# A Strassen feed-forward on one core: block products in another order, a filter tap on ScalarE, a low part on VectorE

## The reference, cut to what matters

```python
def conv_ffn(h, w_in, conv_w, conv_b, w_out, pad):
    T = h.shape[1]
    u = h @ w_in
    up = jnp.concatenate([pad.astype(u.dtype), u], axis=1)
    c = conv_b + sum(up[:, j:j + T] * conv_w[j] for j in range(CONV_W))
    g, val = jnp.split(c, 2, axis=-1)
    y = (jax.nn.silu(g) * val) @ w_out
    return y, up[:, up.shape[1] - (CONV_W - 1):]
```

## Time and profile before

| | |
|---|---|
| median of 3 runs | 3251.47 us (3251.31 to 3253.42) |
| the profiled execution | 3248.83 us, its span 3247.0 us |
| busy share of the span | PE 92%, PEld 89%, DVE 67%, POOL 51%, ACT 38% |
| mean granted TensorE clock | 0.971 |
| feed-forward of layer 0, opening | 732 to 791 us |
| its 20 pairs | 791 to 1256 us |
| its down-projection | from 1262 us |

### The profile page before, as it was taken

How to read it: one execution, slowest core, us unless ns; L and a number is a source line. 1 busy time by engine, 2 the same in 40 slices (tenths; PEclk the granted TensorE clock), 3 DMA queues, 4 the chain that set the end, 5 groups by cost and what they waited for, 6 DMA issues and landing times.

```text
span 3247.0 us, 47471 instructions
## 1 busy us (share of the span) xinstructions
PE 2993.8 (92%) x18469; PEld 2876.1 (89%) x18469; DVE 2178.7 (67%) x3257; ACT 1238.0 (38%) x2590; POOL 1650.1 (51%) x1023
## 2 busy tenths in 40 slices
PE   7999999896999999999987999999699999999998
PEld 6888888796999998999977888889699999999997
DVE  6666666347888887335776777762888888833465
ACT  5555555223333332113340666651333333311243
POOL 2222221325899994222334778753499999622231
PEclk8999999898999999999988999999899999999999
DMA  5222222312222224211104121221122222422111
GB/s 113 69 68 72 68 66 91 104 40 73 70 73 68 73 67 152 101 60 55 39 24 121 34 59 51 94 82 46 64 69 73 70 70 72 156 79 78 59 39 62
DMA packets 284366, 237.37 MB, mean 73 GB/s; under 512 B 29988, under 2 KB 266228, under 8 KB 284148
## 3 DMA queue, kind: packets, MB, share of 16 engines
q1 hardware_dynamic: 269336, 220.43, 22.5%
q10 hardware_dynamic: 14812, 13.97, 1.4%
HBM read 170.20 MB, written 64.16 MB: 72 GB/s over the span
## 4 chain that ended last, share of the span: by engine, by line
PE 61%; DVE 13%; POOL 11%; issue 6%; ACT 5%; DMA 3%; SPq 0%; ACTq 0%; POOLq 0%; DVEq 0%
PE ps L1150 17%; PE ps L1152 16%; PE ps L1151 16%; POOL t L934 6%; PE ps L1333 2%; ACT t L1916 2%; PE ps L1468 2%; PE ps L1286 2%; PE ps L1269 2%; DVE t L2351 1%; POOL t L962 1%; POOL t L953 1%; PE ps L1353 1%; DVE t L2366 1%; DMA t<-in_w_ffn_in 1%
## 5 line engine op out<-in xcount | busy, mean ns | idle before, releaser
L1150 PE MATMUL ps<-t,t 128*128 128x384 f32 (+1 forms) x4760 | 1601.1, 336 | 136.9 <-POOL t L889 53.8
L1152 PE MATMUL ps<-t,t 128*128 128x384 f32 (+1 forms) x4760 | 1566.6, 329 | 0.0
L1151 PE MATMUL ps<-t,t 128*128 128x384 f32 (+1 forms) x4760 | 1565.3, 329 | 0.0
L1150 PEld LDWEIGHTS ps<-t,t 128*128 128x128 f32 x4760 | 903.8, 190 | 177.5 <-POOL t L889 55.5
L1151 PEld LDWEIGHTS ps<-t,t 128*128 128x128 f32 x4760 | 904.8, 190 | 1.0 <-issue 0.2
L1152 PEld LDWEIGHTS ps<-t,t 128*128 128x128 f32 x4760 | 903.2, 190 | 0.0
L934 POOL TENSOR_TENSOR t<-t,t 128x512 fp32r<-128x512 f32 x320 | 542.0, 1719 | 20.0 <-ACT t L2024 10.7
L889 POOL TENSOR_TENSOR t<-t,t 128x1024 fp32r<-128x1024 f32 x101 | 249.0, 2465 | 455.5 <-ACT t L1803 452.2
L2024 ACT ACTIVATE t<-t 128x512 fp32r<-128x512 f32 x320 | 198.0, 631 | 526.8 <-POOL t L942 218.8
L2698 DVE TENSOR_TENSOR t<-t,ps 128x384 f32<-128x384 f32 (+1 forms) x240 | 126.3, 531 | 279.6 <-PE ps L1152 279.6
L883 POOL TENSOR_TENSOR t<-t,t 128x1024 fp32r<-128x1024 f32 x51 | 106.0, 2079 | 266.5 <-PE ps L1152 266.0
(11 more groups left out here) (191 smaller groups left out, 4119.4 us busy)
## 6 DMA issues: line engine op xcount, KB each, us to landing
t<-in_w_ffn_in SPq DMA_DIRECT2D x160, 256.0 KB, 2.9
ff_dram<-t SPq DMA_DIRECT2D x44, 544.0 KB
t<-ff_dram SPq DMA_DIRECT2D x44, 544.0 KB, 6.8
t<-in_w_ffn_out SPq DMA_DIRECT2D x44, 512.0 KB, 3.4
t<-in_w_qkv_a SPq DMA_DIRECT2D x24, 512.0 KB, 3.9
t<-in_w_ple_gate SPq DMA_DIRECT2D x16, 512.0 KB, 3.8
out<-t SPq DMA_DIRECT2D x32, 192.0 KB, 2.1
t<-in_w_o_a SPq DMA_DIRECT2D x8, 512.0 KB, 4.0
```

The lines of the kernel that those rows point to most:

```text
L1150: pe.matmul(out, a_hi, b_hi, start=start, stop=False, skip_group_check=True)
L1151: pe.matmul(out, a_hi, b_lo, start=False, stop=False, skip_group_check=True)
L1152: return pe.matmul(out, a_lo, b_hi, start=False, stop=stop, skip_group_check=True)
```

## The change

- **PE's order in a pair** becomes A11, A11, S3, A21, A22, A22, S2, S1, A12, A12, S4. The steps of `blk_done` are renumbered with it: 4 is A22, 5 is S2, 6 is S1, 7 is A12, 8 is S4.
- **POOL** takes the low part of A22 right after that of A21, before S4; it no longer takes that of A12 (seven low parts in a pair). **DVE** takes it in `last_low`, between the gate filter and the gate. PE's A12 products wait for it.
- **The first tap** of both filters goes to ACT (`first_tap`: Identity with scale and bias over 1090 elements). In ACT's order the value tile's stands behind the highs of A22(n+1) and S2(n+1), the gate tile's at the head of the next pair. ACT's other steps are put in another order too.
- **SP** waits for step 4 (not 6) before it loads A22(n+1) and for step 7 (not 8) before A12(n+1). `store_tile(n + 1)` stays where it is.
- **Opening:** ACT copies and splits in another order, the fourth combination moves from POOL to DVE (`combined_fourth`) with its own buffers for each k (`t4_words`, four counters in place of one), POOL splits chunk c0+2 before it combines.
- **Down-projection:** the first four gated tiles come into `ff_first`, not `ff_raw[0]`, and are loaded after step 4 of the last pair; on DVE they come before the last value filter.

```diff
@@ SP, a pair
                         load_block("A21", n + 1)
                         store_tile(n + 1)
-                        sp.wait_ge(blk_done, BLK_DONE + done + 6)
+                        sp.wait_ge(blk_done, BLK_DONE + done + 4)
                         load_block("A22", n + 1)
-                        sp.wait_ge(blk_done, BLK_DONE + done + 8)
+                        sp.wait_ge(blk_done, BLK_DONE + done + 7)
                         load_block("A12", n + 1)
...
-                        sp.wait_ge(blk_done, BLK_DONE + done + 5)
-                        down_chunk(0, 1)
+                        sp.wait_ge(blk_done, BLK_DONE + done + 4)
                         sp.wait_ge(ff_stored, FF_STORED + 16 * (f0 + 8))
                         load_tiles(0)
+                        sp.wait_ge(blk_done, BLK_DONE + done + 6)
+                        down_chunk(0, 1)
@@ POOL, pair_weights
                 block_rest("A21", 2)
+                block_rest("A22", 4)
                 pool.wait_ge(blk_loaded["A12"], BLK_LOADED + 16 * (m + 1))
...
                 block_rest("S2", 5)
                 block_rest("S1", 6)
-                block_rest("A22", 4)
                 block_rest("S4", 8)
-                block_rest("A12", 7)
@@ POOL, ffn_weights and combine
                 split(c0 + 1, ffn=l)
+                split(c0 + 2, ffn=l)
                 combine(l, 0)
-                combine(l, 1)
-                split(c0 + 2, ffn=l)
-                combine(l, 2)
-                combine(l, 3)
                 split(c0 + 3, ffn=l)
+                for k in range(1, 4):
+                    combine(l, k)
...
+                if k == 3:
+                    stored, before = comb_stored[1]
+                    pool.wait_ge(stored, before + 32 * (l + 1))
...
-                pool.tensor_tensor(t4_raw, h21, t_raw[1][:, k, :], ALU.subtract).then_inc(comb_made, 1)
@@ ACT
+                def first_tap(unit, t, kind):
+                    n = t + NFF * kind
+                    act.wait_ge(pad_done, unit + 1)
+                    if t:
+                        act.wait_ge(ff_made, f0 + t)
+                    act.activation((cg, cv)[kind], ubuf[kind][:, 2:T + 4], ACT.Identity, scale=conv_c[l][:, n + 88:n + 89],
+                                   bias=conv_c[l][:, n + 132:n + 133]).then_inc(conv_step, 1)
@@ ACT, pair (the new order)
                     if n:
                         first_tap(unit - 1, n + 1, 0)
                         first_copied(n)
                         loaded_high("A12", n)
                         made_high("S4", n, 4)
                         sigmoid(n + 1, unit - 1)
                     if more:
                         loaded_high("A11", n + 1)
                         loaded_high("A21", n + 1)
                         made_high("S3", n + 1, 1)
                     act.wait_ge(blk_done, BLK_DONE + 8 * m + 4)
                     last_segment(ubuf[1], 6)
                     if more:
                         loaded_high("A22", n + 1)
                         made_high("S2", n + 1, 2)
                         first_tap(unit, n + 2, 1)
                         made_high("S1", n + 1, 3)
                     act.activation(ubuf[0][:, 2:386], ps[:, 0, 0:384], ACT.Copy).then_inc(u_kept, 1)
                     last_segment(ubuf[0], 5)
@@ DVE, filtered, gate_half and pair
-                    dve.wait_ge(pad_done, unit + 1)
-                    dve.tensor_scalar(dst, ub[:, 2:T + 4], col(88), col(132), ALU.mult, ALU.add).then_inc(conv_step, 1)
                     dve.wait_ge(conv_step, 3 * unit + 1)
...
+                    if n < PAIRS - 1:
+                        last_low(n + 1)
                     gate_tile(2 + n, unit)
...
+                def last_low(n):
+                    m = PAIRS * l + n
+                    hi, lo, raw = slots[l]["A12"]
+                    dve.wait_ge(s_made, S_MADE + 4 * m + 4)
+                    dve.wait_ge(blk_high, BLK_HIGH + 8 * m + 7)
+                    dve.tensor_tensor(lo, raw, hi.bitcast(F32), ALU.subtract).then_inc(sums_made, 1)
@@ DVE, opening (the new order)
                 combined_parts(0)
                 combined_parts(1)
+                filtered(u0, 0, 0, 5)
+                combined_fourth(0)
+                combined_parts(2)
                 combined_low(0)
+                filtered(u0 + 1, 0, 1, 6)
+                combined_fourth(1)
+                combined_parts(3)
                 combined_low(1)
+                combined_fourth(2)
                 combined_low(2)
+                combined_fourth(3)
                 combined_low(3)
                 gate_tile(0, u0 + 1)
                 filtered(u0 + 2, 1, 0, 9)
                 filtered(u0 + 3, 1, 1, 12)
+                last_low(0)
                 gate_tile(1, u0 + 3)
```

More of the change, by code:

```diff
@@ L456, in program @@
         comb_low, COMB_LOW = again(first_added, 9)
[L457 removed]
+        comb_stored = [again(consts_loaded, 96), again(rel_copied, 1), again(qkv_first[1], 16), again(qkv_first[2], 16)]
         t4_loaded, T4_LOADED = again(ident_loaded, 16)
@@ L691, in ffn @@
                 sp.wait_ge(gemm_done, g0 + 8)
-                sp.wait_ge(comb_stored, COMB_STORED + 128 * (l + 1))
+                for stored, before in comb_stored:
+                    sp.wait_ge(stored, before + 32 * (l + 1))
                 sp.dma_start(h_hi[:, 0:4, 384:768].bitcast(F32), t4h_dram).then_inc(t4_loaded, 16)
@@ L2014, in combined_high @@
                 def combined_high(k):
-                    made = 16 * l + 4 * k
+                    made = 12 * l + 3 * k
                     for i, t in enumerate((0, 2, 1)):
@@ L2074, in kept, with first_copied @@
                         last_segment(ub, bank)
+                def first_copied(n):
+                    m = PAIRS * l + n
+                    if n == 0:
+                        stored, before = comb_stored[3]
+                        act.wait_ge(stored, before + 32 * (l + 1))
+                    act.wait_ge(part_done, PART_DONE + 2 * m + 1)
+                    if m:
+                        act.wait_ge(sums_made, SUMS_MADE + 6 * (m - 1) + 2)
+                    act.activation(p1_sum, ps[:, 0, 0:384], ACT.Copy).then_inc(p1_kept, 1)
                 def pair(n):
@@ L2079, in pair @@
                     more = n < PAIRS - 1
-                    act.wait_ge(part_done, PART_DONE + 2 * m + 1)
-                    if m:
-                        act.wait_ge(sums_made, SUMS_MADE + 5 * (m - 1) + 1)
-                    act.activation(p1_sum, ps[:, 0, 0:384], ACT.Copy).then_inc(p1_kept, 1)
-                    loaded_high("A12", n)
-                    made_high("S4", n, 4)
+                    if n:
+                        first_tap(unit - 1, n + 1, 0)
+                        first_copied(n)
+                        loaded_high("A12", n)
+                        made_high("S4", n, 4)
+                        sigmoid(n + 1, unit - 1)
                     if more:
                         loaded_high("A11", n + 1)
+                        loaded_high("A21", n + 1)
+                        made_high("S3", n + 1, 1)
                     else:
@@ L2090, in pair @@
                         weights_high(c0 + 4, 0)
-                    if n:
-                        sigmoid(n + 1, unit - 1)
-                    if more:
-                        loaded_high("A21", n + 1)
-                        made_high("S3", n + 1, 1)
-                    act.wait_ge(blk_done, BLK_DONE + 8 * m + 6)
+                    act.wait_ge(blk_done, BLK_DONE + 8 * m + 4)
                     act.wait_ge(conv_step, 3 * (unit - 1) if n else 3 * unit)
@@ L2100, in pair @@
                         loaded_high("A22", n + 1)
+                        made_high("S2", n + 1, 2)
+                        first_tap(unit, n + 2, 1)
+                        made_high("S1", n + 1, 3)
                     else:
@@ L2603, in combined_parts, with combined_fourth @@
                     p.then_inc(comb_hn, 1)
+                def combined_fourth(k):
+                    dve.wait_ge(comb_made, COMB_MADE + 12 * l + 3 * k + 3)
+                    if k == 2:
+                        stored, before = comb_stored[0]
+                        dve.wait_ge(stored, before + 32 * (l + 1))
+                    dve.tensor_tensor(t4_raw[k], parts[k % 2][2], t_raw[1][:, k, :], ALU.subtract).then_inc(comb_hn, 1)
                 def combined_low(k):
                     done = 16 * l + 4 * k
-                    dve.wait_ge(comb_made, COMB_MADE + done + 4)
                     for i, t in enumerate((0, 2, 1)):
```

159 lines of the change are left out of this document (81 added, 78 removed).

## The result

The changed kernel takes 3319.61 us (median of four runs, 3317.75 to 3322.99), the kernel before, in the same runs, 3251.84 us: a ratio of 1.0209, 95% interval 1.0191 to 1.0226. The forecast was 3303 us, 3215 to 3335. The profiled execution has a span of 3321.2 us against 3247.0, at a mean granted clock of 0.964 against 0.971.

What follows compares the result with a forecast made beforehand. A new dependency cycle through SP, POOL, ACT and DVE was to bound the pairs: 809 + 19 x 24.6 + 11 = 1287.4 us, 25.7 later per layer; 3251.5 + 51.4 = 3303 us, range 3215 to 3335.

Steps and rivals of the forecast that it cites:

- old cycle: Pairs before the change: S2 and A22 products on PE, load, POOL's sums and low parts, S2 again; period 23.12 us.
- new cycle: Pairs: gate's end, store, A22 load, S2, its high, value tap, DVE, next gate; period 24.6 us, chance 0.66.
- the closing: Last gate to the down-projection: tiles loaded directly behind the store, down-projection 11 us behind the gate, 14.6 before.
- less 1.0: Taken off the pair's sum of 25.6 us, as POOL is not in DVE's way for every long operation.
- step 3: Value tile's second and third tap on DVE, both beside POOL's work: 2 x 2.27, 4.54 us.
- step 7: The gate on DVE at the end of a pair's turn: 5.82 us.
- step 5: Gate tile's first tap on ACT, 1.19 us, then its two taps on DVE, 4.54 us.
- step 1: Gate's end to A22 landed: issue behind the store 0.5, load to S2 2.95, store's packets 0.8; 4.2 us.
- the ring: Dependency loop of one pair over SP, POOL, ACT and DVE, passing to DVE by the value tap; 24.6 us a turn.
- PE as the bound: Rival: the stop before S2 goes and PE sets a period of 21.8 us; 3197 us, chance 0.22.
- Tables on ACT: Rival: Identity needs another table, two loads of 2.56 us a turn; 3400 us, chance 0.06 shared with other cases.
- the gain of the opening: Rival: pair 0's loads and tile 1's gate come 20 us earlier; 3263 us, chance 0.06 shared with other cases.

Runs made afterwards that it cites:

- e1: Changed kernel with SP issuing the load of A22(n+1) before the store of tile n+1: 3200.31 us, ratio to before 0.9842.
- e10: Changed kernel with SP waiting for the gate's end, then issuing the load of A22(n+1) and the store behind it: 3296.01 us.
- e2: Changed kernel with the value tile's first tap on ACT put before the highs of A22(n+1) and S2(n+1): 3293.69 us.
- e5: Changed kernel with both first taps of the pairs back on DVE, SP's order unchanged: 3314.08 us.
- e6: Changed kernel with value tap and copies of banks 0 and 5 before the next pair's highs on ACT, load still behind the store: 3235.23 us.
- e7: Kernel before the change, with the load of A22(n+1) put before the store of tile n+1 on SP: 3254.28 us, ratio 1.000.
- e9: e1 with loads also put before stores in the opening, the fourth combination stored in four parts: 3181.8 us.
- e11: e9 with the four down-projection tiles also loaded before the last pair's store: 3171.31 us, ratio to before 0.9747.
- e8: Changed kernel with the load of A22(n+1) before the store and both first taps of the pairs on DVE: 3234.74 us.

## Why the prediction was right, and where it was off

**Direction, size and place were right.** The time lies in the range, 17 us over the forecast. In the profiled layer 0 the down-projection begins 10.5 us later than forecast: 4.1 in the 19 periods, 2.5 in the start, 1.4 from there to the gate of tile 1, 2.5 in the closing. (Two slips in the prediction's arithmetic change nothing in this: the ends of its range stand on the profiled execution, 3248.8, and the forecast on the median, 3251.5, on which they would be 3270 and 3337; and the terms of the opening that lead to 788 add up to 786.8.) That the old cycle is cut holds: PE no longer stops for S2, and with the queue reordered the same kernel is bound by PE at 21.68 us in a pair (21.8 was read off before). That a new cycle closes through `store_tile`, the load of A22, POOL's S2 and ACT holds too, and e1 shows it. By the same run the rest of the change is worth 51 us, and the order on SP takes these back and 68 more.

**The steps of the cycle**, from 938.20 to 963.11 in the rows above:

| step | forecast | measured |
|---|---|---|
| 1 gate's end to S2 | 4.2 | 3.98 |
| 2 S2, high, tap | 3.05 | 3.17 |
| 3 second and third tap | 4.54 | 4.07 |
| 4 last sum and pad | 1.1 | 1.30 |
| 5 gate tile's taps | 5.73 | 5.94 |
| 6 sigmoid, low part inside | 1.18 | 1.71 |
| 7 gate | 5.82 | 4.74 |
| sum | 25.6, less 1.0 | 24.91 |

That the sum came within 0.3 us is in part luck, as terms of 0.5 to 1.1 us are off both ways. The tap takes 1.28 to 1.31 us, not the sigmoid's 1.11, and it stands twice in a turn. A12's low part beside POOL took 1.78 and hence was not covered by the sigmoid: 0.5. POOL out of DVE's way gave 0.47 in step 3 and 1.08 in step 7, and the tails and the taps of step 5, beside POOL, gave some of it back. In step 1 the store in front of the load was priced at 0.8 for packets; the load takes 0.57 longer from its issue to S2 with the store in front (e10). The ring order that the Trainium skill states (DMA: Bandwidth & Descriptors, section "Queues, rings and completion order") agrees in sign with this: 3.57 against 3.00.

**The step that failed is the reason, not the number: the tap as the only link.** The prediction let the ring pass from ACT to DVE by the value tile's tap alone, and said that before the change no operation of DVE stood behind A22. That was wrong by the order of the kernel before: ACT's copies of banks 0 and 5, which DVE's gate filter needs, stood behind the highs of A22 and S2 there too. They only had room, as the copy of bank 0 in the kernel before shows: 0.64 us of idle time, ended by PE and not by the high.

```profile
859.51 0.63 ACT L2024 ACTIVATE t<-t 128x512 fp32r<-128x512 f32 x1 [2.00 <-DMA t<-in_w_ffn_in]
860.78 0.49 ACT L2106 ACTIVATE t<-ps 128x384 f32<-128x384 f32 x1 [0.64 <-PE ps L1152]
```

In the changed kernel the copies of banks 0 and 5 stand behind the same waiting high, and now it comes last. With the tap moved (e2) or gone (e5) the ring closes over PE's A11 and DVE's sums, or over DVE's gate filter, at 24.3 and 24.75; only when the copies are moved as well (e6) does the period fall to 22.6. So the forecast of 24.6 came out although a cure drawn from it, moving the tap, would have brought 26 us of 119.

**PE's stop** was forecast in front of S4, 2.8 us. It is in front of A11, released by ACT's L2132, 2.35 on average (40.0 in 17), by the link that the prediction left out: the copy stands behind the waiting high. That a slower clock behind it uses up the next stop held in the pairs shown: 2.95, then 1.60.

**Opening and closing.** From DVE's first work to the gate of tile 1 the sum was right to 1.4 us (77.7 against 76.3), but the start was already 2.5 us later than before. That much lies between single executions: e7, which up to there is the kernel before, starts at 738.78, 6.0 us later than the profiled execution of the kernel before (732.75), and e1, which up to there is the changed kernel, at 734.19 against its 735.28. The loads of pair 0 came at 778.10 (773 forecast), A12(0) at 800.45 (797). Timelines of the kernel after, SP and POOL:

```profile
767.63 0.43 SPq L687 DMA_DIRECT2D t_low_dram<-t  x1
...
777.62 0.43 SPq L687 DMA_DIRECT2D t_low_dram<-t  x1
778.10 1.62 SPq L658 DMA_DIRECT2D t<-in_w_ffn_in  x3
...
771.83 1.01 POOL L924 TENSOR_TENSOR t<-t,t 128x384 f32<-128x384 f32 x1 [13.85 <-DMA t_low_dram<-t]
...
800.45 1.28 POOL L967 TENSOR_TENSOR t<-t,t 128x512 f32<-128x512 f32 x1 [7.35 <-DMA t<-in_w_ffn_in]
```

Of the 5.1 us of the loads, 2.2 are the later end of `combined_low(1)` (767.2 for 765), 2.1 the wait for its store (4.56 us, from the first store's issue at 767.27 to POOL's start at 771.83, where I took the 2.45 of the earlier trace rows), and 0.8 the issue of the fourth combination's own two stores in front of the loads, which I had left out. In the opening PE stops for 6.4, 10.6 and 4.7 us where it had stopped for 13.8 and 12.3 (both in the earlier trace rows). The closing took 13.5 us and not 11. ACT's Identity brought no table load: in the layer's opening and pairs the trace has a single ACT_TABLE_LOAD at the sigmoid, at 784.19, as before, and two taps run ahead of it. With the Trainium skill (ScalarE: Activation LUTs, section "Table sets: the hidden batching unit") the trace agrees.

**The rivals.** PE as the bound (3197) was the right account of the change without its queue: e1 gives 3200.31. Its chance of 0.22 rested on POOL leaving DVE alone; what it needed was one line of SP. That POOL keeps meeting DVE does not hold this rival back: at 21.68 us they have room for it. Tables on ACT did not come, and the gain of the opening did not either; e9 shows what was to be had there, 18.5 us in both layers together, and e11 another 10.5 in front of the down-projection.

## What to carry to other kernels

On a queue that works in order, a transfer whose own condition is met early must not stand behind one that waits for late work; when a wait is made earlier, read first what stands in front of it, since the order that was free before (e7, ratio 1.000) can then cost more than the change gains (e1, 119 us). When a ring runs through an engine that works in order, everything behind its waiting instruction is a link: list all of it, as cutting one link (e2, e5) moves the wait and leaves the period. A move of work that brings nothing measurable inside a ring (the taps in e5) can be worth something once it is cut (34 us in e8), so the ring is to be cut first and the parts judged after.

## What the runs showed of the hardware

- DVE and POOL slow each other's operations by an amount that hardly depends on their length: a tap took 1.35 or 2.27 us, a multiplication of 64 elements 0.21 (at 962.90) or 1.31, and the filter's two multiplications of two elements 0.23 or 1.34 (at 950.60). Small operations lose as much as long ones, 0.9 to 1.1 us; POOL's 512-element sum took 1.29 alone and 2.26 beside DVE (e6, 953.20).
- PE's granted clock went to 0.53 behind a stop of 2.95 us (872 to 875) and 0.50 behind one of 3.64 (e2, 970 to 973), and stayed at 1.00 behind one of 1.60 (896.70 to 899), but also behind one of 2.99 (1094.60 to 1098.00). The next stop was shorter behind the slow stretches and not behind the last.
- ACT's Identity with a factor and an addend per partition took 1.28 to 1.31 us over 1090 elements, the sigmoid over as many 1.11.
